# Layers written out instead of looped, and small VectorE operations given to ScalarE, in a two-layer decoder step

## The chip, the cores and the metric

The kernel runs on one core of one Trainium2 chip. The metric is the device time of one execution in microseconds (us). The engines are TensorE (PE in the profile; PEld is its weight load), VectorE (DVE), ScalarE (ACT), GpSimd (POOL) and SyncE (SP, which only issues DMAs). Each has its own instruction stream; they meet at semaphores.

## The reference

One inference step of a decoder of two layers for 256 prompt tokens and 8 sequences of 4 new tokens, 288 columns in all, model width 1024, fp32:

```python
for l in range(DEPTH):                       # DEPTH = 2
    z = x @ w_in                             # conv branch and attention branch
    u = ua * sigmoid(ug)                     # GLU, 512 channels
    A = silu(layer_norm(depthwise_conv31(u))) @ w_conv_out
    B = gated_sum(compressed, selected, window attention) @ w_attn_out
    m = sigmoid(g_a) * A + sigmoid(g_b) * B
    x = layer_norm(ALPHA * x + m @ w_o)
    x = layer_norm(ALPHA * x + (silu(x @ w_gate) * (x @ w_up)) @ w_down)
```

The old K and V rows lie in pages that a page table picks; the new K, V and convolution rows are outputs too.

## The kernel before

Everything is kept with channels on partitions and the 288 tokens as columns. Each fp32 operand of a big product is split into a rounded part and a rest (`w_hi`, `w_lo`; `x_hi`, `x_lo`), and a product is three matmuls (lines 717 to 719, 735 to 737, 754 to 756). Weights come in chunks of 128 x 1024: SyncE loads a chunk into one of three slots (`load_chunk`), ScalarE rounds it into `w_hi` (`high_part`, line 1129), GpSimd takes the rest into `w_lo` (`low_part`, four instructions of line 640), TensorE uses it. There are three `w_hi`/`w_lo` slots, so rounding chunk n waits until TensorE has finished chunk n-3.

**Order of work.** No planner: each engine's stream is written out by hand for one layer, and TensorE, VectorE, ScalarE and GpSimd run it in a hardware loop of two passes (`with layers(...)`, lines 647, 963, 1308, 1850). SyncE's stream has one pass in a loop and one behind it (lines 601 to 605). In a loop each `wait_ge` compares a semaphore with a value worked out from the register `layer`, and semaphores count on through both layers.

**First stage of a layer** (outputs 0 to 7 of `project_x`). TensorE multiplies the not yet normalised `xr_hi`/`xr_lo`, and VectorE corrects each result by mean and deviation. The outputs alternate between two PSUM banks, and output n+2 waits until VectorE has read output n out of its bank (line 1858). In VectorE's stream (lines 1886 to 1919) `norm_pair` normalises the residual, `fix_gate(c)` makes the gate's argument and `take_u(c)` makes `u`; ScalarE takes the tanh of the gate in between (`gate`, line 1333). `low_features` makes `x_lo`. Then come small operations on the layer's vectors `sm`: `nsa_hi`, `half_gb`, `alpha_gb` and two extra columns of `x_hi` (lines 1907 to 1918). After them VectorE works on the depthwise convolution (`convolve`, line 1602), with rotary steps between (`rope`, lines 1929 to 1936, which wait for TensorE's `turn`, line 996).

**Compression stage.** For five groups of rows (4, 0, 1, 2, 3, in this order) TensorE multiplies (`compress`, line 819), ScalarE copies half of the result (`h1_copy`), VectorE and ScalarE go to and fro for a GELU (`compress_dve`, line 1611, and `gelu_act`), and TensorE multiplies by the second weight (`second`, lines 833 to 840). On ScalarE the last group's `h1_copy(layer, 3)` (line 1399) stands behind copies into `v_tok` and `v_misc` and the DMA `kv_out` (lines 1389 to 1398). On TensorE two whole outputs (`fill`) stand between the fourth group's compression and `second(layer, 3)`; convolution statistics (line 774) follow. VectorE then copies the new tokens' queries into `qs_raw` and `qs_rot`, 16 copies of 64 x 32 (line 1952), which the attention over old rows needs first at line 913.

Of the kernel before, what the change touches and what calls it, by code (L numbers as in the profile page):

```python
# [19 lines left out]
F32 = mybir.dt.float32  # L20
# [9 lines left out]
TOKX = TOK + 2  # L30
# [117 lines left out]
def decoder_kernel(nc, xT, consts, page_table, weights, small, w1, w2, cmp_pages, slc_pages, win, past_u,  # L148
                   yT, kv_out, p_conv_out, s_conv_out, win_out):
    with ExitStack() as ctx:  # L150
# [141 lines left out]
        def s(name):  # L292
            return sm[:, SMALL[name]]
# [121 lines left out]
        rstd_copied = Signal("rstd_copied", 1)  # L415
        gate_fixed = Signal("gate_fixed", KC)
# [70 lines left out]
        def layers(eng):  # L487
            return eng.Fori(0, DEPTH)
# [5 lines left out]
        def _(sp):  # L494
# [107 lines left out]
            with sp.Fori(0, DEPTH - 1) as layer:  # L602
                body(layer, True)
                lead(layer + 1, False)
# [14 lines left out]
        def _(pool):  # L619
# [27 lines left out]
            with layers(pool) as layer:  # L647
# [39 lines left out]
        def _(pe):  # L687
# [275 lines left out]
            with layers(pe) as layer:  # L963
# [146 lines left out]
        def _(act):  # L1110
            owned = (act_order, conv_hi_ready, attn_hi_ready, hid_hi_ready, gates_act, hi_ready, x_hi_ready, gates_read, xc_ready, v_ready, h1_ready, hsq_ready, hth_ready, cmp_ready, squared, mean_squared, mean_copied, sd_ready,
                     swish_ready, gexp1, gwin_ready, gexp2, gpt_act, uexp, upt_ready, ax_ready, x_ready, ffn_tanh, raw_hi_ready, rstd_copied, gate_tanh)
# [195 lines left out]
            with layers(act) as layer:  # L1308
# [24 lines left out]
                def gate(n):  # L1333

                    act.wait_ge(*gate_fixed(layer, n + 1))
                    if n >= 2:
                        act.wait_ge(*u_taken(layer, n - 1))
                    do(sig_u[:, n % 2], gate_ps, ACT.Tanh, gate_tanh, wait=False, scale=0.5, bias=sums_of[:, 2, n % 2:n % 2 + 1])
# [18 lines left out]
                features_rounded(layer, 3)  # L1357
                chunk_read(4)
# [38 lines left out]
                act.wait_ge(*roped(layer, 2))  # L1397
# [158 lines left out]
        def _(dve):  # L1556
            v = nc.vector
            owned = (dve_order, conv_lo_ready, attn_lo_ready, hid_lo_ready, nsa_ready, x_lo_ready, x_sum, conv_ready, roped, qs_ready, hs_ready, hin_ready, hg_ready, centered, shifted, var_ready, sum_ready, square_sum_ready, normed, conv_act, gate_normed, hid_ready,
# [291 lines left out]
            with layers(dve) as layer:  # L1850
# [10 lines left out]
                def fix_gate(c):  # L1861

                    unshift_raw(2 * c, sums_of[:, 0])
                    do(v.tensor_scalar(sums_of[:, 2, c % 2:c % 2 + 1], sums_of[:, 0, 1:2], 0.5, None, ALU.mult), wait=False)
                    do(v.tensor_tensor(gate_ps, fixed_ps, rstd_sb, ALU.mult), gate_fixed)

                def take_u(c):

                    unshift_raw(2 * c + 1, sums_of[:, 1])
                    do(v.tensor_tensor(fixed_ps, fixed_ps, rstd_sb, ALU.mult))  # L1870
                    dve.wait_ge(*gate_tanh(layer, c + 1))
                    su = sig_u[:, c % 2]
                    do(v.tensor_scalar(su, su, 0.5, 0.5, ALU.mult, ALU.add))
# [33 lines left out]
                do(v.tensor_copy(nsa_hi[:], nsa_f))  # L1907
# [3 lines left out]
                do(v.tensor_scalar(half_gb[:], sm[:, SMALL["cg"].start:SMALL["cb"].stop], 0.5, None, ALU.mult))  # L1911
                do(v.tensor_scalar(alpha_gb[:], sm[:, SMALL["g1"].start:SMALL["b1"].stop], ALPHA, None, ALU.mult))
                g1, b1 = s("g1").unsqueeze(2), s("b1").unsqueeze(2)
                do(v.tensor_scalar(x_hi[:, :, TOK:TOK + 1], g1, -1.0, None, ALU.mult), wait=False)
                do(v.tensor_copy(x_hi[:, :, TOK + 1:TOKX], b1))
# [32 lines left out]
                for gg in range(2):  # L1948
                    rows = slice(64 * gg, 64 * gg + 64)
                    for src, dst in ((q_raw, qs_raw), (q_rot, qs_rot)):  # L1950
                        for hh in range(HG):
                            i = v.tensor_copy(dst[rows, :, gg, hh], src[rows, hh, SEQ:TOK].rearrange("p (b t) -> p b t", b=DEC_B))
                            do(i, qs_ready if gg and dst is qs_rot and hh == HG - 1 else None, wait=False)
# [122 lines left out]
                def raw_columns():  # L2076
# [156 lines left out]
```

## Time and profile before

| what | value |
|---|---|
| three runs | 1010.43, 1012.06, 1014.05 us (median 1012.06) |
| profiled execution | 1015.24 us |
| its span, first to last instruction | 1013.4 us |
| TensorE busy | 961.2 us (95%) |
| GpSimd busy | 752.4 us (74%) |
| VectorE busy | 653.0 us (64%) |
| ScalarE busy | 536.4 us (53%) |
| mean granted TensorE clock | 0.985 |

The shares are averages over a kernel with many stages. An engine that is busy for 95% of the span is the one to follow: what matters is where it isn't busy, what it waited for there, and where its clock was granted at half.

### The profile page before, as it was taken

To read this page: it belongs to the slowest core of one execution; us is meant where nothing else is said; L and a number is where in the kernel's file an instruction comes from. 1 tells how busy PE (TensorE), PEld (TensorE's weight loads), DVE (VectorE), ACT (ScalarE), POOL (GpSimd) and SP (SyncE) were. 2 spreads that over 40 slices of the span, in tenths; PEclk is the share of its full clock that TensorE was granted. 3 is DMA by queue.
4 is the path that set the end of the run, shared out by engine and by line. 5 is a ranking of instruction groups with operands and counts; after the bars stand their busy time and mean duration, and the time that the engine had idled before them with its cause. 6 is when DMAs were issued, how large, how long until landed. Compare 5 with 4: busy or idle time off the path is not lost.

```text
span 1013.4 us, 23246 instructions
## 1 busy us (share of the span) xinstructions
PE 961.2 (95%) x7294; PEld 912.0 (90%) x7294; DVE 653.0 (64%) x1476; ACT 536.4 (53%) x1000; POOL 752.4 (74%) x1081
## 2 busy tenths in 40 slices
PE   6898999989999999999989989999899999999995
PEld 5897888878999999999989978898799999999994
DVE  7999766566687555531469995855676765556035
ACT  5452475545575555544464426764556555555355
POOL 7787746443978888898877786455269888888986
PEclk9998999999999999999989999999999999999998
DMA  8885686822456764555457566776134454555543
GB/s 294 276 252 182 196 251 220 308 92 63 129 173 205 237 201 163 166 183 170 147 182 237 164 200 174 264 237 221 54 98 159 143 161 160 166 167 168 174 159 110
DMA packets 78916, 185.08 MB, mean 183 GB/s; under 512 B 9538, under 2 KB 42690, under 8 KB 78530
## 3 DMA queue, kind: packets, MB, share of 16 engines
q1 hardware_dynamic: 70288, 167.03, 50.6%
q10 hardware_dynamic: 8354, 15.59, 4.5%
q8 instruction: 62, 1.02, 0.4%
q0 software_dynamic: 144, 0.89, 0.2%
q14 instruction: 68, 0.56, 0.2%
HBM read 170.90 MB, written 12.57 MB: 181 GB/s over the span
## 4 chain that ended last, share of the span: by engine, by line
POOL 54%; issue 23%; PE 20%; ACT 1%; POOLq 1%; DVE 1%; DMA 0%; ACTq 0%; SPq 0%; DVEq 0%
POOL w_lo L640 47%; PE proj L717 5%; PE proj L718 4%; PE proj L719 4%; POOL hid L665 3%; POOL res L663 3%; PE proj L735 2%; PE proj L736 2%; PE proj L737 2%; DMA res<-xT_in 0%; POOLq L660 0%; POOLq L634 0%; ACT res L1134 0%; ACT xr_hi L1120 0%; POOL res L673 0%
## 5 line engine op out<-in xcount | busy, mean ns | idle before, releaser
L640 POOL TENSOR_TENSOR w_lo<-wch,w_hi 128x256 fp32r<-128x256 f32 x940 | 685.2, 764 | 245.2 <-ACT w_hi L1129 244.6
L717 PE MATMUL proj<-x_hi,w_hi 128*128 128x290 f32 (+1 forms) x1120 | 340.8, 304 | 2.8 <-ACT hid L1142 2.6
L718 PE MATMUL proj<-x_hi,w_lo 128*128 128x290 f32 (+1 forms) x1120 | 332.9, 297 | 0.0
L719 PE MATMUL proj<-x_lo,w_hi 128*128 128x290 f32 (+1 forms) x1120 | 332.1, 296 | 0.0
L1129 ACT ACTIVATE w_hi<-wch 128x1024 fp32r<-128x1024 f32 x235 | 247.8, 1055 | 130.1 <-PE proj L737 74.5
L717 PEld LDWEIGHTS proj<-x_hi,w_hi 128*128 128x128 f32 x1120 | 211.7, 189 | 6.6 <-issue 4.0
L718 PEld LDWEIGHTS proj<-x_hi,w_lo 128*128 128x128 f32 x1120 | 212.3, 190 | 0.6
L719 PEld LDWEIGHTS proj<-x_lo,w_hi 128*128 128x128 f32 x1120 | 212.3, 190 | 0.0
L735 PE MATMUL proj<-hid_hi,w_hi 128*128 128x288 f32 x352 | 104.3, 296 | 0.0
L737 PE MATMUL proj<-hid_lo,w_hi 128*128 128x288 f32 x352 | 103.6, 294 | 0.0
L736 PE MATMUL proj<-hid_hi,w_lo 128*128 128x288 f32 x352 | 103.3, 293 | 0.0
L1602 DVE SCALAR_TENSOR_TENSOR ps_s<-u_p,sm,ps_s 128x256 f32<-128x256 f32 x232 | 94.1, 483 | 3.8
L1688 DVE SCALAR_TENSOR_TENSOR res<-proj,res 128x288 f32<-128x288 f32 x32 | 14.6, 455 | 107.9 <-PE proj L737 93.0
L2096 DVE COPY sums_of<-proj 128x2 f32<-128x2 f32 x88 | 14.1, 160 | 95.3 <-PE proj L719 95.0
L736 PEld LDWEIGHTS proj<-hid_hi,w_lo 128*128 128x128 f32 x352 | 66.2, 188 | 0.1
L735 PEld LDWEIGHTS proj<-hid_hi,w_hi 128*128 128x128 f32 x352 | 66.1, 188 | 0.1
L737 PEld LDWEIGHTS proj<-hid_lo,w_hi 128*128 128x128 f32 x352 | 66.1, 188 | 0.0
L1134 ACT ACTIVATE q_raw<-q_raw,sums_of 128x288 f32<-128x288 f32 x44 | 23.6, 537 | 74.1 <-DVE q_raw L2109 74.1
L717 PE MATMUL proj<-xr_hi,w_hi 128*128 128x290 f32 x128 | 41.1, 321 | 17.6 <-POOL w_lo L640 9.7
L1134 ACT ACTIVATE res<-res,unit_top 128x128 f32<-128x128 f32 (+2 forms) x96 | 37.6, 393 | 27.7 <-DVE unit_top L1756 27.5
L717 PEld LDWEIGHTS proj<-xr_hi,w_hi 128*128 128x128 f32 x128 | 26.3, 205 | 19.2 <-DVE xr_lo_a L1578 9.7
L718 PE MATMUL proj<-xr_hi,w_lo 128*128 128x290 f32 x128 | 40.0, 312 | 0.0
(319 smaller groups left out, 1761.2 us busy)
## 6 DMA issues: line engine op xcount, KB each, us to landing
wch<-weights_in SPq DMA_DIRECT2D x235, 512.0 KB, 3.7
pg<-slc_pages_in SPq DMA_DIRECT2D x128, 128.0 KB, 2.4
pg<-cmp_pages_in SPq DMA_DIRECT2D x96, 128.0 KB, 3.1
wn<-win_in SPq DMA_DIRECT2D x16, 512.0 KB, 5.5
win_out<-wn ACTq DMA_DIRECT2D x4, 2048.0 KB, 9.7
pg<-cmp_pages_in ACTq DMA_DIRECT2D x32, 128.0 KB, 3.3
hid<-w_in SPq DMA_DIRECT2D x2, 1024.0 KB, 5.6
kv_out<-kv ACTq DMA_DIRECT2D x2, 864.0 KB, 4.4
```

Of the source, the lines that this page charges most:

```text
L640: last = nc.gpsimd.tensor_tensor(lo[:, cols], raw[:, cols], hi[:, cols].bitcast(F32), ALU.subtract)
L663: do(nc.gpsimd.tensor_tensor(dst, u_s[:, :, :, tap:tap + DEC_T], tap_weight(conv_w[:, :, tap]), ALU.mult))
L665: do(nc.gpsimd.tensor_tensor(out, out, tap_s[:], ALU.add))
L717: mm(ps, hi[:, kb], x_h[:, 0:n], start=kb == 0, stop=False)
L718: mm(ps, lo[:, kb], x_h[:, 0:n], start=False, stop=False)
L719: last = mm(ps, hi[:, kb], x_l[:, 0:n], start=False, stop=kb == KD - 1)
L735: mm(ps, hi, hid_hi[:, kb], start=kb == 0, stop=False)
L736: mm(ps, lo, hid_hi[:, kb], start=False, stop=False)
L737: last = mm(ps, hi, hid_lo[:, kb], start=False, stop=kb == KF - 1)
L1129: hi_ready.up(nc.scalar.activation(w_hi[:, n % PAIRS].rearrange("p k n -> p (k n)"), wch[:, n % SLOTS].rearrange("p k n -> p (k n)"), ACT. ...
L1134: i = nc.scalar.activation(out, in_, func, **kw)
L1602: i = v.scalar_tensor_tensor(out=out, in0=in_, scalar=conv_w[:, c, tap:tap + 1], in1=so_far, op0=ALU.mult, op1=ALU.add)
```

## The change

The four loops become Python loops, so that each engine's stream holds both layers one behind the other, and every wait compares with a constant. SyncE's loop of one pass is written out too. Counters of the signals are set back at each layer. In the first stage and behind the compression, work of VectorE goes to ScalarE. The halvings in `u` are arranged anew: ScalarE makes `1 + tanh` and VectorE multiplies by half of the deviation; to match, the extra column b2 of `xr_hi` is stored halved.

```diff
-        def layers(eng):
-            return eng.Fori(0, DEPTH)
+        def layers(signals):
+
+            for layer in range(DEPTH):
+                for sig in signals:
+                    sig.count = 0
+                yield layer
...
-            with sp.Fori(0, DEPTH - 1) as layer:
+            for layer in range(DEPTH - 1):
...
-            with layers(act) as layer:
+            for layer in layers(owned):
...
                 def gate(n):
...
-                    do(sig_u[:, n % 2], gate_ps, ACT.Tanh, gate_tanh, wait=False, scale=0.5, bias=sums_of[:, 2, n % 2:n % 2 + 1])
+                    do(sig_u[:, n % 2], gate_ps, ACT.Tanh, scale=0.5, bias=sums_of[:, 0, 1:2])
+                    do(sig_u[:, n % 2], sig_u[:, n % 2], ACT.Identity, gate_tanh, wait=False, bias=1.0)
...
                 features_rounded(layer, 3)
+                act.wait_ge(*small_in(layer, 1))
+                nsa_f = s("nsa").rearrange("p (c w) -> p c w", c=KD)
+                do(nsa_hi[:], nsa_f, ACT.Copy, wait=False)
+                do(x_hi[:, :, TOK:TOK + 1], s("g1").unsqueeze(2), ACT.Copy, wait=False, scale=-1.0)
+                do(x_hi[:, :, TOK + 1:TOKX], s("b1").unsqueeze(2), ACT.Copy, wait=False)
+                do(half_gb[:], sm[:, SMALL["cg"].start:SMALL["cb"].stop], ACT.Copy, wait=False, scale=0.5)
+                do(alpha_gb[:], sm[:, SMALL["g1"].start:SMALL["b1"].stop], ACT.Copy, small_copied, scale=ALPHA)
                 chunk_read(4)
...
-                act.wait_ge(*roped(layer, 2))
+                act.wait_ge(*roped(layer, 6))
+                for gg in range(2):
+                    rows = slice(64 * gg, 64 * gg + 64)
+                    for src, dst in ((q_raw, qs_raw), (q_rot, qs_rot)):
+                        for hh in range(HG):
+                            do(dst[rows, :, gg, hh], src[rows, hh, SEQ:TOK].rearrange("p (b t) -> p b t", b=DEC_B), ACT.Copy,
+                               qs_ready if gg and dst is qs_rot and hh == HG - 1 else None, wait=False)
...
                 def fix_gate(c):
...
-                    do(v.tensor_scalar(sums_of[:, 2, c % 2:c % 2 + 1], sums_of[:, 0, 1:2], 0.5, None, ALU.mult), wait=False)
...
                 def take_u(c):
...
-                    do(v.tensor_tensor(fixed_ps, fixed_ps, rstd_sb, ALU.mult))
+                    do(v.scalar_tensor_tensor(out=fixed_ps, in0=fixed_ps, scalar=0.5, in1=rstd_sb, op0=ALU.mult, op1=ALU.mult))
                     dve.wait_ge(*gate_tanh(layer, c + 1))
                     su = sig_u[:, c % 2]
-                    do(v.tensor_scalar(su, su, 0.5, 0.5, ALU.mult, ALU.add))
...
-                do(v.tensor_copy(nsa_hi[:], nsa_f))
+                dve.wait_ge(*small_copied(layer, 1))
                 do(v.tensor_tensor(nsa_lo[:], nsa_f, nsa_hi[:].bitcast(F32), ALU.subtract), nsa_ready)
                 fix_gate(3)
                 take_u(3)
-                do(v.tensor_scalar(half_gb[:], sm[:, SMALL["cg"].start:SMALL["cb"].stop], 0.5, None, ALU.mult))
-                do(v.tensor_scalar(alpha_gb[:], sm[:, SMALL["g1"].start:SMALL["b1"].stop], ALPHA, None, ALU.mult))
                 g1, b1 = s("g1").unsqueeze(2), s("b1").unsqueeze(2)
-                do(v.tensor_scalar(x_hi[:, :, TOK:TOK + 1], g1, -1.0, None, ALU.mult), wait=False)
-                do(v.tensor_copy(x_hi[:, :, TOK + 1:TOKX], b1))
...
                 compress_dve(layer, 3, fill=6)
-                for gg in range(2):
-                    rows = slice(64 * gg, 64 * gg + 64)
-                    for src, dst in ((q_raw, qs_raw), (q_rot, qs_rot)):
-                        for hh in range(HG):
-                            i = v.tensor_copy(dst[rows, :, gg, hh], src[rows, hh, SEQ:TOK].rearrange("p (b t) -> p b t", b=DEC_B))
-                            do(i, qs_ready if gg and dst is qs_rot and hh == HG - 1 else None, wait=False)
                 conv_center(layer)
...
-                    do(v.tensor_copy(xr_hi[:, :, TOK + 1:TOKX], b2))
+                    do(v.tensor_scalar(xr_hi[:, :, TOK + 1:TOKX], b2, 0.5, None, ALU.mult))
...
-                        do(v.tensor_tensor(lo[:, :, TOK + 1:TOKX], b2[:, blocks], xr_hi[:, blocks, TOK + 1:TOKX].bitcast(F32), ALU.subtract),
-                           wait=False)
+                        do(v.scalar_tensor_tensor(out=lo[:, :, TOK + 1:TOKX], in0=b2[:, blocks], scalar=0.5,
+                                                  in1=xr_hi[:, blocks, TOK + 1:TOKX].bitcast(F32), op0=ALU.mult, op1=ALU.subtract), wait=False)
```

## Rows read from the trace of the kernel before

**Rows 1.** The page's first part: busy time and share of each engine.

```profile
PE 961.2 (95%) x7294; PEld 912.0 (90%) x7294; DVE 653.0 (64%) x1476; ACT 536.4 (53%) x1000; POOL 752.4 (74%) x1081
```

**Rows 2.** The waits of TensorE: us in total, times, longest us.

```profile
PE proj L717 <- POOL w_lo L640: 11.1, 4, 9.7
PE ps_o L833 <- DVE res L1650: 5.2, 2, 2.6
...
PE proj L717 <- issue: 4.0, 1, 4.0
PE proj L717 <- DVE ps_t L1858: 4.0, 4, 1.5
```

**Rows 3.** Timeline between the layers: start, length, engine, line, operation, [idle before].

```profile
505.40 0.65 PE L796 MATMUL ps_s<-sq,cst 128*128 128x288 f32 x2
510.05 0.60 PE L717 MATMUL proj<-xr_hi,w_hi 128*128 128x290 f32 x1 [4.00 <-issue]
...
507.49 1.96 DVE L2128 RECIPROCAL ps_w<-sq 128x288 f32<-128x288 f32 x1 [0.60 <-ACT sq L1134]
513.12 0.76 DVE L1727 SCALAR_TENSOR_TENSOR res<-ps_s,res 128x576 f32<-128x576 f32 x1 [3.67 <-issue]
...
510.01 0.20 ACT L1134 ACTIVATE warm<-eps 128x1 f32<-128x1 f32 x1
...
510.47 2.79 POOL L640 TENSOR_TENSOR w_lo<-wch,w_hi 128x256 fp32r<-128x256 f32 x4
```

**Rows 4.** Busy time by stretch; PEclk is the granted clock, 1.00 the full one.

```profile
93.00:100.00 7.00, 6.46 (x20) 5.17 (x21) 6.74 (x18) 0.69 (x2) 5.98 (x14) 0.51 0.27 81
...
509.00:516.00 7.00, 5.95 (x24) 5.96 (x25) 1.97 (x3) 1.62 (x3) 4.25 (x6) 0.53 0.51 167
516.00:520.00 4.00, 4.00 (x31) 4.00 (x31) 3.16 (x8) 3.32 (x7) 2.18 (x4) 0.97 0.11 39
```

**Rows 5.** First stage of layer 0: timeline rows, and one group of small operations.

```profile
33.49 0.40 PE L717 MATMUL proj<-xr_hi,w_hi 128*128 128x290 f32 x1 [1.11 <-DVE ps_t L1858]
38.50 0.39 PE L717 MATMUL proj<-xr_hi,w_hi 128*128 128x290 f32 x1 [1.52 <-DVE ps_t L1858]
...
19.82 3.33 DVE L1873 TENSOR_SCALAR sig_u<-sig_u 128x288 f32<-128x288 f32 x1
27.94 0.31 DVE L1873 TENSOR_SCALAR sig_u<-sig_u 128x288 f32<-128x288 f32 x1
...
26.76 0.48 ACT L1134 ACTIVATE sig_u<-ps_t,sums_of 128x288 f32<-128x288 f32 x1
...
L1912 DVE TENSOR_SCALAR alpha_gb<-sm 128x16 f32<-128x16 f32 x2 | 1.3, 663 | 0.1
```

**Rows 6.** Timeline of layer 0 ahead of the compression: the fourth turn and its use.

```profile
82.92 0.65 PE L996 MATMUL ps_t<-q_raw,cst 128*128 128x288 f32 x2
...
84.39 0.45 DVE L1934 TENSOR_TENSOR sig_u<-ps_t,cst 128x288 f32<-128x288 f32 x1
```

**Rows 7.** Timeline of layer 0 around the last compression group.

```profile
119.03 2.04 ACT L1134 ACTIVATE v_misc<-ps_t 32x1024 f32<-32x1024 f32 x2
121.86 0.77 ACT L1134 ACTIVATE res<-ps_w 64x128 f32<-64x128 f32 x4 [0.79 <-PE ps_w L819]
...
127.25 0.68 DVE L1653 SCALAR_TENSOR_TENSOR res<-sq 64x512 f32<-64x512 f32 x1
...
128.40 0.44 PE L837 MATMUL ps_o<-res,w_sb 64*64 64x128 f32 x4
```

**Rows 8.** Groups of small ScalarE operations: busy us, mean ns of one, idle before.

```profile
L1134 ACT ACTIVATE kp_cmp<-ps_o 64x16 f32<-64x16 f32 x4 | 0.7, 178 | 0.4 <-ACT sq L1134 0.3
L1134 ACT ACTIVATE res<-ps_w 64x128 f32<-64x128 f32 x16 | 3.1, 271 | 3.9 <-PE ps_w L819 3.1 <-ACT v_misc L1134 0.8
L1134 ACT ACTIVATE warm<-eps 128x1 f32<-128x1 f32 x10 | 2.0, 203 | 0.1
```

**Rows 9.** The group of VectorE's query copies, same columns.

```profile
L1952 DVE COPY qs_raw<-q_raw 64x32 f32<-64x32 f32 x16 | 1.8, 173 | 0.1
```

More of the change, by code:

```diff
@@ L415, in decoder_kernel @@
         rstd_copied = Signal("rstd_copied", 1)
+        small_copied = Signal("small_copied", 1)
         gate_fixed = Signal("gate_fixed", KC)
@@ L646, in _ @@
             lo_ready.count = 0
-            with layers(pool) as layer:
+            for layer in layers((pool_order, lo_ready, conv_s_ready, half_centered)):
                 for n in range(PAIRS, EARLY + PAIRS):
@@ L961, in group_turn @@
                 gout_turned.up(pe.transpose(ps_o[:, P:2 * P], group_rows, k("ident")))
-            with layers(pe) as layer:
+            owned = (out_done, down_used, gates_turned, gout_turned, gates_done, turned, v_turned, h_done, w2_done, stat_done, spread_done, gm_done, gs_done, gsum_done, gt_done, gpv_done, us_done, ut_done, upv_done)
+            for layer in layers(owned):
                 state["out"] = 0
@@ L1111, in _ @@
             owned = (act_order, conv_hi_ready, attn_hi_ready, hid_hi_ready, gates_act, hi_ready, x_hi_ready, gates_read, xc_ready, v_ready, h1_ready, hsq_ready, hth_ready, cmp_ready, squared, mean_squared, mean_copied, sd_ready,
-                     swish_ready, gexp1, gwin_ready, gexp2, gpt_act, uexp, upt_ready, ax_ready, x_ready, ffn_tanh, raw_hi_ready, rstd_copied, gate_tanh)
+                     swish_ready, gexp1, gwin_ready, gexp2, gpt_act, uexp, upt_ready, ax_ready, x_ready, ffn_tanh, raw_hi_ready, rstd_copied, gate_tanh, small_copied, qs_ready)
             for sig in owned + (out_read[0], out_read[1], kv_stored, conv_stored, win_stored):
@@ L1307, in _ @@
             act.wait_ge(table_in, 16)
-            with layers(act) as layer:
+            for layer in layers(owned):
                 now["layer"] = layer
@@ L1557, in _ @@
             v = nc.vector
-            owned = (dve_order, conv_lo_ready, attn_lo_ready, hid_lo_ready, nsa_ready, x_lo_ready, x_sum, conv_ready, roped, qs_ready, hs_ready, hin_ready, hg_ready, centered, shifted, var_ready, sum_ready, square_sum_ready, normed, conv_act, gate_normed, hid_ready,
+            owned = (dve_order, conv_lo_ready, attn_lo_ready, hid_lo_ready, nsa_ready, x_lo_ready, x_sum, conv_ready, roped, hs_ready, hin_ready, hg_ready, centered, shifted, var_ready, sum_ready, square_sum_ready, normed, conv_act, gate_normed, hid_ready,
                      spread_read, gneg1, gm_read, gimp, gneg2, gp_ready, gpt_dve, gcopy_ready, go_ready, us_read, uneg, up_ready, uo_ready, mixed_ready, raw_lo_ready, sm_free, rstd_ready, gate_fixed, u_taken)
@@ L1848, in group_out @@
                     do(v.tensor_copy(dst, src), go_ready if g else None)
-            with layers(dve) as layer:
+            for layer in layers(owned):
                 now["layer"] = layer
```

## Prediction

> **What bounds the kernel.** First the engines' shares: TensorE is busy for 961.2 us of a span of 1013.4 [rows 1]. Some 52 us are left in which it stands still, and other engines count only where they cause these. Second, TensorE's waits [rows 2]: 9.7 of the 11.1 us for `w_lo` are the start of the kernel, which the change leaves as it is. The waits that the change touches are one of 4.0 us "for issue", in which nothing that the profile shows was missing; four, 4.0 us in all, for VectorE reading a bank (line 1858); and two, 5.2 us in all, for the first compression group (line 1650). Third, the timeline between the layers [rows 3]: the only "issue" wait is the loop's jump back. TensorE's last matmuls of layer 0 end at 506.05, the next starts at 510.05. VectorE stood 3.67 us after its reciprocal, also for "issue". Fourth, the granted clock [rows 4]. After the jump it was at half: 24 matmuls in 5.95 us between 509 and 516, against 31 in 4.00 us between 516 and 520. At 0.129 us each, 24 would take 3.1 us, so the low clock cost 2.9 us there. A like stretch follows the compression wait of layer 0 (0.51 from 93 to 100).
>
> **The jump.** With both layers written out there is no jump. The 4.0 us go if all that output 0 needs is there at 506.05: its weights were rounded before, and the last `xr_lo` block, which is not much later, is for the last eighth of the output only. So output 0 starts at once: -4.0. TensorE doesn't stand still, so I take the clock as staying at full: -2.9. What is late next is chunk 2. Its `w_lo` runs on GpSimd from 510.47 to 513.26 [rows 3], behind GpSimd's own subtraction, and none of that came from the jump. Outputs 0 and 1 (24 matmuls each at 0.135 us, some 3.25 us an output) end at 512.6, so TensorE waits 0.7 us. VectorE gets only 3.6 us earlier while TensorE gets 6.9 us earlier. I laid VectorE's steps of the first stage out again from 509.5 on with their old lengths less what is removed: output 6 starts without a wait, output 7 waits 0 to 1.4 us for its bank, as the four `low_features` ahead of it take very different times in the two layers. That is 0.7 in the middle, plus 0.3 for small ones, against 0.8 of wait there before (one of the four of [rows 2]): +0.2. ScalarE's restart, just after 510.21, is in time for all of this. Sum: -4.0 - 2.9 + 0.7 + 0.2 = -6.0. Ends: -2 (clock not regained, chunk 2 and 7 late) and -7.5 (no new wait). The waits' constants cost TensorE nothing: their arithmetic ran beside the queued matmuls, and is put at 0.
>
> **First stage, layer 0.** VectorE loses line 1873, four times 0.31 us, but one of them took 3.33 us at 19.82 [rows 5], four tiny ones of line 1864, and `nsa_hi`. ScalarE gains an Identity of about the tanh's length, 0.5 us, behind a finished tanh. The 3.0 us of the long one don't come through: the next `take_u` needs ScalarE's second tanh, which ran from 26.76 to 27.24, so the Identity ends near 27.9, where VectorE was at 27.94 anyhow. What is left is 0.31 a time: the waits of 1.11 and 1.52 us [rows 5] shrink together by 0.7. Taken: -0.7. Ends: -2.5 (nearly all of both) and +0.6 (the Identity late in each gate).
>
> **Small operations on `sm`.** Off VectorE come four at 0.2 to 0.7 us in the row of line 1912 and its neighbours, and `nsa_hi`; ScalarE gets five, some 0.2 us each by [rows 8], 1.1 us in all. They stand ahead of rounding chunk 7, and `w_lo` of chunk 7 would end about when output 7 starts: hidden, just. VectorE's new wait for them is met long before; behind it is only `nsa_lo`, which TensorE needs after output 7. VectorE's relief, 4 us by then, is mostly not worth its length either: its third and fourth `rope` need TensorE's turns. The fourth turn ended at 83.57 and VectorE used it at 84.39 [rows 6], so VectorE can gain 0.7 us on TensorE and no more. Both compression waits (2.6 us each, [rows 2]) shrink by that: -1.4. Ends: 0 and -1.4, and the half clock behind them may go as well (below). `raw_columns` keeps its count and shapes of instructions: 0.
>
> **The 16 copies on ScalarE.** They go ahead of `h1_copy(layer, 3)`. In layer 0 ScalarE's `v_misc` copies end at 121.07, `h1_copy(3)` starts at 121.86, VectorE's last step for this group ends at 127.93, and TensorE takes it at 128.40, right behind its two fills [rows 7]. So the slack is about 0.3 us. The new `roped(6)` wait costs 0: VectorE's `rope(5)` comes before its `compress_dve(2)`, thus before ScalarE's part of that group, which is before the copies. A 64x32 copy has no row: between 178 ns (64x16) and 271 ns (64x128), and 203 ns for a single column [rows 8]. Four of the 271 ns took 0.77 us, so they overlap, 0.17 apart. Taken 0.16 apart, 2.6 us for 16. Up to 0.3 us of it lies under the 0.79 us that ScalarE waited there. That leaves 2.3, less 0.3 of slack: 2.0 us of new TensorE wait in each layer, since convolution statistics and attention all stand behind it. VectorE's own copies, 173 ns each and overlapped [rows 9], lay ahead of `conv_center`, where it waits for TensorE: their going gives 0. Queued behind the copies are also `kv_out` (nobody waits for it soon) and the reading of two fills, first needed after `second(3)`. +4.0. Ends: +1.0 a layer (0.1 apart) and +3.7 a layer (0.25 apart, one after another), +2.0 and +7.4.
>
> A rule of the Trainium skill speaks against this part: "VectorE: DVE Perf Modes", section "The TRN2 errata", gives a ScalarE operation from SBUF to SBUF 224 cycles plus its elements, which would be an estimate of 213 ns a copy and 3.4 us for 16 without overlap. By it the term would be +5.6 rather than +4.0.
>
> **Sum.** -6.0 - 0.7 - 1.4 + 4.0 = -4.1 us. The profiled execution took 1015.24 (span 1013.4), 3.2 above the median of the three runs; a difference carries over, so 1012.06 - 4.1 = 1008.0.
>
> **Rivals.** The measurement tells 0.3%, 3.0 us, from no change.
>
> (a) The copies are hidden, or cheap, and a half-clock stretch behind a shortened wait goes. For it: the overlap at 0.17. Against: slack of 0.3 only. Copies +2.0, clock -2.9: near 1003. Chance 0.2.
>
> (b) The 4.0 us aren't the jump's: some other thing is late and the wait only changes its name. For it: "issue" names no cause. Against: VectorE shows it at the same place [rows 3], and TensorE in its whole trace nowhere else [rows 2]. Then -2.1 + 4.0, about 1014: no change. Chance 0.1.
>
> The Trainium skill, "Runtime: NRT & Kernel Launch", section "Instruction fetch mechanics", says that a taken branch outside the held pages makes the engine fetch before it can go on; by that rule (b) falls, and the trace's one "issue" wait agrees.
>
> (c) The clock moves about: a new wait of 2 us behind the fills is followed by half clock in one layer, +2.9. For it: of two equal waits before line 833 each was followed by some. Near 1011. Chance 0.12.
>
> (d) Slower: the copies run one after another, 3.7 us of wait a layer, and each such wait brings a half-clock stretch of 2.9 us: +13.2 against -8.1, 1017. It decides from some 0.25 us a copy on. For it: TensorE's longest other waits are shorter than 3.7. Against: ScalarE's small copies overlap. Chance 0.07.
>
> My forecast has the other 0.51. The range leaves out (d) and the tails: 1002.5 to 1013. Faster by over 0.3% are the forecast for the most part, (a), and a few of (c): 0.61. Same: the rest of the forecast, (b), most of (c): 0.32. Slower: 0.07.
>
> **What would show it.** Right: TensorE's waits have no "issue" row of 4 us; the clock at the layer boundary stays at 1.00; a short wait for `w_lo` at output 2 of layer 1; a new wait of about 2 us before line 837 in both layers, released by VectorE's line 1653, with `h1_copy(3)` as much later; compression waits of 1.9 rather than 2.6 us. Wrong: no wait at line 837 (copies hidden), or over 3 us there; a low clock at the boundary in spite of no standstill; a rise of the waits for `w_lo` in the first stage, which would mean that ScalarE's new work holds up the rounding of weights.

## The result and the profile after

The changed kernel takes 1002.95 us (median, 1002.45 to 1003.35), the kernel before beside it 1013.05: ratio 0.9898, 95% interval 0.9877 to 0.9918, so 10 us less, where 4.1 were forecast. The direction was right, and the time lies inside the range by 0.45 us at its lower end, but the size was less than half of what came. Of the four terms behind it one came out, and that one in part by luck, as is shown below. The profiled execution took 1003.35 us with a span of 1001.6, against 1015.24 and 1013.4 before.

The page's first part says where the 11.8 us of span came from: against [rows 1] TensorE's busy time fell by only 2.1 us, so 9.7 us are standstill.

```profile
PE 959.1 (96%) x7294; PEld 908.8 (91%) x7294; DVE 634.5 (63%) x1418; ACT 544.7 (54%) x1050; POOL 752.9 (75%) x1081
```

TensorE's waits in the changed kernel, same columns as [rows 2]:

```profile
PE proj L722 <- POOL w_lo L645: 13.8, 7, 9.9
PE ps_o L966 <- DVE sq L1857: 4.1, 2, 2.1
PE ps_o L842 <- DVE res L1673: 3.4, 4, 0.9
PE ps_s L941 <- DVE res L1772: 2.3, 2, 1.1
PE proj L722 <- ACT hid L1148: 1.8, 2, 0.9
PE ps_o L838 <- DVE res L1670: 1.2, 2, 0.7
PE ps_s L918 <- DMA pg<-slc_pages_in: 0.9, 1, 0.9
```

The "issue" row is gone. The two waits of 2.6 us for the first compression group (L833, now L838) are 1.2 us in all. The waits for VectorE's reading of a bank, 4.0 us before, have left the list, in part for waits for `w_lo` (11.1 to 13.8). The forecast new wait before the last compression group is there, but short: of the four waits of L842, two of 0.8 to 0.9 us stand before the first group that uses it and two, 0.89 and 0.73 us, before the last.

The clock by stretch, columns as [rows 4]; first fence the profiled execution of the changed kernel, second that of the same program run again later (below):

```profile
93.00:100.00 7.00, 6.16 (x37) 5.11 (x36) 6.83 (x16) 2.99 (x11) 6.06 (x13) 1.00 0.90 277
219.00:227.00 8.00, 8.00 (x45) 6.75 (x45) 4.74 (x16) 3.59 (x20) 0.00 (x0) 0.59 0.01 2
509.00:516.00 7.00, 6.85 (x51) 6.88 (x52) 5.16 (x12) 5.22 (x11) 6.25 (x10) 1.00 0.70 201
707.00:712.00 5.00, 5.00 (x33) 4.01 (x32) 3.79 (x10) 2.35 (x11) 0.00 (x0) 0.67 0.07 27
```

```profile
219.00:227.00 8.00, 6.92 (x58) 5.61 (x58) 6.08 (x17) 4.35 (x15) 0.58 (x1) 1.00 0.00 0
707.00:712.00 5.00, 4.09 (x34) 3.32 (x33) 3.97 (x11) 1.77 (x10) 0.00 (x0) 1.00 0.01 2
```

The stretches at 1.2 GHz of [rows 4], behind the compression wait and behind the jump, are at the full 2.4 GHz now. Two others came up behind the wait of 2.06 us before L966 in both layers, and the second execution has not even those.

**The positions.** Nothing so far says which part of the change did it. For that I read when TensorE starts the same matmul in both traces. Position is start in microseconds, in the timeline:

| TensorE's work | before | after | gained in the stage | forecast |
|---|---|---|---|---|
| layer 0: end of the first stage (start of `nsa`) | 42.27 | 38.77 | 3.50 | 0.7 |
| layer 0: first compression group (L833/838) | 93.54 | 87.94 | 2.10 | part of 1.4 |
| layer 0: next group (L837/842) | 104.55 | 96.88 | 2.07 | 0 |
| layer 0: last group (L837/842) | 128.40 | 121.66 | -0.93 | -2.0 |
| layer 0: last matmuls (L796/801) | 505.40 | 500.97 | -2.31 | 0 |
| layer 1: end of the first stage | 539.71 | 529.24 | 6.04 | 6.0 |
| layer 1: first compression group | 590.94 | 578.59 | 1.88 | part of 1.4 |
| end of TensorE's work | 1000.89 | 989.17 | -0.63 | -2.0 |

In these two traces the boundary came out as forecast to the tenth, the copies at less than half, and the first stage and the compression groups at several times their terms. The last row holds more than the copies of layer 1: 0.66 us are gained up to the next group, 0.70 lost up to the last (at 624.56 before and 612.25 after), and 0.59 lost behind it. The 2.07 us of the third row are the half clock of [rows 4] from 93 to 100, priced there by the like stretch at 2.9, less a new wait of 0.84. Of the 2.31 us lost in the fifth, 1.60 are in this execution alone, with its low clock from 219 to 226; the second execution, which has no low clock there, still loses 0.71, although the kernel before had 3.4 us of half clock in the same stage (154.4 to 157.8). Nothing here places this remainder.

### The profile page after: what moved, and what is told of

It reads as the page before. It is cut to its first block, busy times and chain, and to the rows that moved or that the text cites. A ratio compares the mean times of both kernels' runs of the same rounds, so it can differ in the third digit from the quotient of the medians.

```text
span 1001.6 us, 21268 instructions
## 1 busy us (share of the span) xinstructions
PE 959.1 (96%) x7294; PEld 908.8 (91%) x7294; DVE 634.5 (63%) x1418; ACT 544.7 (54%) x1050; POOL 752.9 (75%) x1081
## 4 chain that ended last, share of the span: by engine, by line
PE 72%; DVE 8%; ACT 6%; SPq 5%; POOL 4%; issue 3%; DMA 2%; ACTq 0%; DVEq 0%
PE proj L722 16%; PE proj L723 15%; PE proj L724 15%; PE proj L740 5%; PE proj L741 5%; PE proj L742 5%; POOL w_lo L645 3%; ACT res L1140 3%; SPq L518 2%; SPq L532 2%; PE ps_o L891 1%; ACT w_hi L1135 1%; PE proj L759 1%; DMA wch<-weights_in 1%; DVE ps_s L1622 1%
## 5 line engine op out<-in xcount | busy, mean ns | idle before, releaser
L1140 ACT ACTIVATE hid_hi<-ps_s 128x288 fp32r<-128x288 f32 x44 | 18.1, 411 | 43.5 <-DVE ps_s L2128 43.5
L722 PE MATMUL proj<-mix_hi,w_hi 128*128 128x288 f32 x128 | 38.2, 298 | 1.6 <-POOL w_lo L645 1.6
```

The costliest lines, as they stand in the source:

```text
L722: mm(ps, hi[:, kb], x_h[:, 0:n], start=kb == 0, stop=False)
L1140: i = nc.scalar.activation(out, in_, func, **kw)
```

## The experiments

**The theories.** A, the one on record: the layer jump carries the gain and the waits' constants are worth nothing. B: with the layers written out each wait's value is a constant, which was expected to shorten every hand-over between VectorE and ScalarE by a tenth of a microsecond or two, and to pay where TensorE waits for a chain of them. C came up when the first traces were compared: where the half-clock stretches lie, and a long instruction or two, are accidents of one execution.

All ratios are to runs of the kernel before on the same chip. It took 1012.41, 1014.40 and 1013.73 us in the three sets (the first four runs, the next four, the last four).

### The two halves of the change alone

**The loops written out, nothing else.**

```
-        def layers(eng):
-            return eng.Fori(0, DEPTH)
+        def layers(signals):
+            for layer in range(DEPTH):
...
```

> The kernel before with its loops written out and nothing else. Theory A (the prediction's: writing out saves the jump alone, register arithmetic of the waits costs nothing): -6.0 us, all of it between the layers; the first stage of layer 0 and the waits before lines 833 (2.6 us), 936 (1.13) and 961 (2.33) stay as before. Theory B (each hand-over between engines also gets some 0.1 us shorter, since the wait's value no longer has to be worked out): -7.5 to -9 us, the wait before 961 falls to about 2.06 in both layers and the first stage of layer 0 gets shorter too.

Measured: 1005.48 us, ratio 0.9937 (0.9918 to 0.9957). That is 6.4 us less, between the two theories, and the interval holds both.

**The small operations moved, every loop kept.** The diff is the change without the lines above.

> The changed kernel with its loops kept: only the moved operations. Theory A: -5 us (3.5 in the first stage of layer 0, 1.4 or more before line 833, less 1 us a layer for the query copies), the wait of 4.0 us for issue and the half clock behind it stay. Theory B: -2 to -4 us, because part of what the first stages gained in the changed kernel is due to the constants; the wait before 961 stays 2.33. Rival: the copies on ScalarE eat it up, within 1 us of no change.

Measured: 1014.02 us, ratio 1.0009 (0.9990 to 1.0027). Neither theory had this; the rival came nearest.

Each alone does about what the terms of the forecast say: 6.4 us for the loops (forecast: the boundary's 6.0), and nothing measurable for the small operations (forecast: -0.7, -1.4 and +4.0, some 2 us slower). Together they do 10.3 by the same kind of ratio. The halves' ratios add to 0.9946, give or take 0.0027, where the whole has 0.9898: some 5 us, give or take 3, come only with both. So most of the miss is in having added terms from a trace in which VectorE and ScalarE were late. TensorE's waits with the loops alone written out:

```profile
PE ps_o L965 <- DVE sq L1842: 4.1, 2, 2.1
PE ps_o L837 <- DVE res L1655: 3.1, 2, 1.6
PE proj L721 <- DVE ps_t L1863: 1.9, 2, 0.9
PE ps_o L841 <- DVE res L1658: 1.8, 2, 0.9
```

The wait before the first compression group is 1.6 us here, not 2.6, with no operation taken from VectorE, and the one before the turn of the gate's outputs (L961 before, L965 here) is 2.06 instead of 2.33. That is what B says and A doesn't. The first stage of layer 0 ends at 38.54, ahead of any jump, where it ended at 42.27 before and at 40.18 in another kernel with loops and the same instructions up to there (the copies alone moved, below).

### Which engine's loop

**TensorE's loop alone put back.**

```
-            for layer in layers(owned):
+            with loops(pe) as layer:
                 state["out"] = 0
```

> The changed kernel with TensorE's loop alone kept. If TensorE's own jump is what stands between the layers: the 4.0 us wait for issue is back, a stretch at half clock behind it (2.9 us), minus the 1.1 us wait for w_lo that the changed kernel has there: +5 to +6 us against the changed kernel, thus near 1008.5. If the other engines' jumps set it: within 1.5 us of the changed kernel (1003), with less than 1 us for issue.

Measured: 1005.44 us, ratio 0.9932 (0.9911 to 0.9953). The wait for issue came back, but the time lies between the two that were expected, 1008.5 and 1003.

**VectorE's and ScalarE's loops alone put back.**

```
-            for layer in layers(owned):
+            with loops(act) as layer:
...
-            for layer in layers(owned):
+            with loops(dve) as layer:
```

> The changed kernel with the loops of VectorE and ScalarE alone put back; TensorE, GpSimd and SyncE stay written out. Theory B (the constants in the waits of VectorE and ScalarE carry most of the gain, since each hand-over between them is shorter; TensorE's own jump is worth about 4 us of idle time): the kernel with TensorE's loop alone put back took 1005.4 us and the one with all loops put back 1014.0, so this one has TensorE's jump gone (no wait named issue at 498 to 508 us), but VectorE's jump of 3.7 us is back and TensorE waits some of it out behind the boundary, and the chain of waits before the turn of the gate's outputs is 2.5 us again, not 2.06: 1008 to 1012 us. Theory A (TensorE's jump alone carries the gain, as forecast): no more than 1 us above the changed kernel, 1003 to 1004 us, with that chain at 2.06 us.

Measured: 1015.46 us, ratio 1.0015 (0.9998 to 1.0032): the whole gain is gone, although TensorE has no jump; this is more than B expected. First fence TensorE, second VectorE of this kernel at the boundary, third TensorE with only its own loop back:

```profile
513.46 0.41 PE L724 MATMUL proj<-xr_hi,w_hi 128*128 128x290 f32 x1 [3.33 <-DVE ps_t L1880]
```

```profile
511.15 0.76 DVE L1749 SCALAR_TENSOR_TENSOR res<-ps_s,res 128x576 f32<-128x576 f32 x1 [4.00 <-issue]
```

```profile
502.02 0.60 PE L724 MATMUL proj<-xr_hi,w_hi 128*128 128x290 f32 x1 [4.11 <-issue]
```

TensorE's 4.11 us come back with its loop. Without it, and with VectorE's, TensorE starts the next layer at once (503.36) and then stands 3.33 us for a bank that VectorE reads late, because VectorE itself jumped for 4.00 us. From the last matmuls of layer 0 to the end of layer 1's first stage it takes 34.31 us before, 33.45 with all loops and the small operations moved, 33.02 with TensorE's loop alone, 32.69 with VectorE's and ScalarE's, and 28.27 with none (28.76 in the second execution). The two jumps overlap: take either away and 0.4 to 0.8 us are gained, take both and some 5. The small differences are no more than two executions differ by: the kernel before with the query copies alone moved (below) takes 33.00 us here, against 34.31, with 3.4 us of half clock at the boundary against 6.8. Writing out every loop but TensorE's (1.0009 to 0.9932) gains 7.8 us, most of it within the layers: the next stage shows a part. GpSimd's and SyncE's loops are in this, too, but with VectorE's and ScalarE's kept, writing out the other three gains nothing (1.0015). My term for the boundary came near because I had laid VectorE's steps out without its jump as well; by "TensorE's 4.0 us of issue" alone it would have been wrong.

The Trainium skill, "Runtime: NRT & Kernel Launch", section "Instruction fetch mechanics", has a taken branch outside the held pages cost the engine a fetch. The rows agree that the engine stands at its jump, for 3.67 to 4.13 us on either engine; they don't show what it does in that time.

### The stage between the first stage and the compression

This stretch shows where the halves meet. TensorE needs, from the start of `nsa` to the first compression group:

| kernel | layer 0 | layer 1 |
|---|---|---|
| before | 51.27 | 51.23 |
| small operations moved, all loops kept | 49.50 | 51.27 |
| the same, TensorE's loop written out | 49.41 | 51.18 |
| loops written out alone | 50.25 | 50.28 |
| changed kernel, TensorE's loop put back | 49.30 | 49.25 |
| changed kernel | 49.17 | 49.35 |

In layer 0 the halves give 1.8 and 1.0 us, and together 2.1. In layer 1 they give nothing and 1.0, and together 1.9. Over both layers that is 3.7 against 4.0, so the greater part of what comes only with both lies elsewhere, for some 2.4 us in the query copies (below); the rest isn't placed.

Small operations moved, with loops: VectorE in layer 1, at the fourth turn.

```profile
574.90 3.23 DVE L1624 SCALAR_TENSOR_TENSOR ps_s<-u_p,sm,ps_s 128x256 f32<-128x256 f32 x8
578.04 0.45 DVE L1950 TENSOR_TENSOR sig_u<-ps_t,cst 128x288 f32<-128x288 f32 x1
578.41 0.93 DVE L1951 TENSOR_TENSOR q_rot<-q_raw,cst 128x288 f32<-128x288 f32 x1
579.37 0.86 DVE L1952 TENSOR_TENSOR q_rot<-q_rot,sig_u 128x288 f32<-128x288 f32 x1
```

The changed kernel, VectorE in layer 0 at the same place and on to the first compression group:

```profile
80.10 0.46 DVE L1948 TENSOR_TENSOR sig_u<-ps_t,cst 128x288 f32<-128x288 f32 x1 [0.89 <-PE ps_t L1002]
80.48 0.45 DVE L1949 TENSOR_TENSOR q_rot<-q_raw,cst 128x288 f32<-128x288 f32 x1
80.96 0.46 DVE L1950 TENSOR_TENSOR q_rot<-q_rot,sig_u 128x288 f32<-128x288 f32 x1
84.90 0.52 DVE L1642 SCALAR_TENSOR_TENSOR sq<-ps_w,h_bias,res 64x30 f32<-64x30 f32 x2
85.45 0.88 DVE L1622 SCALAR_TENSOR_TENSOR ps_s<-u_p,sm,ps_s 128x256 f32<-128x256 f32 x2
86.24 0.33 DVE L1662 SCALAR_TENSOR_TENSOR sq<-sq 64x64 f32<-64x64 f32 x1
86.60 0.88 DVE L1622 SCALAR_TENSOR_TENSOR ps_s<-u_p,sm,ps_s 128x256 f32<-128x256 f32 x2
```

And the same steps before:

```profile
84.75 0.84 DVE L1935 TENSOR_TENSOR q_rot<-q_raw,cst 128x288 f32<-128x288 f32 x1
85.62 0.87 DVE L1936 TENSOR_TENSOR q_rot<-q_rot,sig_u 128x288 f32<-128x288 f32 x1
90.06 0.52 DVE L1622 SCALAR_TENSOR_TENSOR sq<-ps_w,h_bias,res 64x30 f32<-64x30 f32 x2
90.69 0.88 DVE L1602 SCALAR_TENSOR_TENSOR ps_s<-u_p,sm,ps_s 128x256 f32<-128x256 f32 x2
91.48 0.28 DVE L1642 SCALAR_TENSOR_TENSOR sq<-sq 64x64 f32<-64x64 f32 x1
91.91 0.88 DVE L1602 SCALAR_TENSOR_TENSOR ps_s<-u_p,sm,ps_s 128x256 f32<-128x256 f32 x2
```

Three things are to be seen. First, in the changed kernel VectorE waits 0.89 us for TensorE's turn: it has caught up, as forecast, and 0.8 us is all that this can give. Behind its own jump, in layer 1 with loops, it isn't caught up: no wait before 578.04, although TensorE's fourth turn was over at 577.31, and the small operations taken off it buy nothing. Second, the two `q_rot` steps take 0.45 and 0.46 us instead of 0.84 and 0.87, another 0.8 us that no term had. GpSimd's rows tell what the earlier steps miss: before, its subtractions for `w_lo` (L640) run from 84.55 to 85.28 and from 85.23 to 86.17, and each step starts beside one of them and ends 0.31 or 0.32 us behind it. After, the steps start at 80.48 and 80.96, in a pause of GpSimd from 78.61 to 81.05. The same holds throughout: in the traces of all 14 runs, 93 rotary steps take over 0.8 us, and every one ends 0.31 to 0.32 us behind a GpSimd instruction that was running when it started. Third, the gap behind a VectorE instruction when the next one waits for a semaphore that is already met: 90.58 to 90.69 and 91.76 to 91.91 before, 85.42 to 85.45 and 86.57 to 86.60 after, 0.11 and 0.15 us against 0.03 each. In each gap of before, VectorE's queue has one register operation (at 90.61 and 91.81, 0.04 us each), and after it has none. That is what the constant saves, some 0.1 us a gap. It is VectorE's own restart that got shorter and not the way over to ScalarE, as B had it: ScalarE starts 0.09 us behind the signal in both (90.58 to 90.67, and 85.42 to 85.51). From the fourth turn's end to the first compression group it was 9.97 us (83.57 to 93.54) and is 7.87 (VectorE's start at 80.10, less the 0.03 of a gap, to 87.94): 2.1 us less, of which 0.8 the earlier start, 0.8 `q_rot`, and 0.5 these gaps and VectorE's shorter last `res` step.

### The query copies

**The copies alone moved, in the kernel before.**

```
-                act.wait_ge(*roped(layer, 2))
+                act.wait_ge(*roped(layer, 6))
+                for gg in range(2):
...
+                            do(dst[rows, :, gg, hh], src[rows, hh, SEQ:TOK]..., ACT.Copy, ...)
```

> The kernel before, with its loops, and of the change the move of the 16 query copies to ScalarE alone. As forecast, 2.0 us per layer at the wait before the last turn of compression, which goes from 0.3 to 1.6 or more, less what VectorE's relief gives later in the layer: 1012 to 1017 us, with that wait at 1.6 us as in the kernel with all the small operations and the loops. Rival (the copies are no part of that 1.6 us; the gate's operations on ScalarE delay it): the wait stays under 0.5 us and the time is that of before, 1013.

Measured: 1016.08 us, ratio 1.0018 (1.0001 to 1.0035). ScalarE's and TensorE's rows at the last group of layer 0, and below them the changed kernel's:

```profile
118.21 0.59 ACT L1134 ACTIVATE qs_raw<-q_raw 64x32 f32<-64x32 f32 x4
120.38 0.77 ACT L1134 ACTIVATE res<-ps_w 64x128 f32<-64x128 f32 x4
126.60 0.43 PE L837 MATMUL ps_o<-res,w_sb 64*64 64x128 f32 x4 [1.59 <-DVE res L1659]
```

```profile
113.27 0.59 ACT L1140 ACTIVATE qs_raw<-q_raw 64x32 f32<-64x32 f32 x4
114.85 0.56 ACT L1140 ACTIVATE qs_rot<-q_rot 64x32 f32<-64x32 f32 x4
115.44 0.77 ACT L1140 ACTIVATE res<-ps_w 64x128 f32<-64x128 f32 x4
121.66 0.43 PE L842 MATMUL ps_o<-res,w_sb 64*64 64x128 f32 x4 [0.89 <-DVE res L1673]
```

The copies take 2.14 us for 16 in both, from the first start to the last end, 0.134 us a copy where I took 0.16. From `h1_copy(3)` to TensorE's use it is 6.22 us in both, and was 6.54 before (121.86 to 128.40, [rows 7]): a slack of 0.32, as forecast. In the kernel with loops the copies make a wait of 1.59 us, and against the kernel before, the stretch from the first use of L837 to the last grows by 1.67 us in layer 0 and 2.15 in layer 1: the forecast's 2.0 a layer. In the changed kernel ScalarE starts them just ahead of TensorE's third group (113.27 against 113.31), where with loops it starts 0.66 us behind it (118.21 against 117.55). ScalarE is earlier in its chain by that much, and so the wait is 0.7 us shorter. Against the loops alone written out (23.84 us from the first use to the last in both layers) the copies cost 0.94 and 0.80 us in the changed kernel (24.78 and 24.64). With all small operations and the loops it is 26.00 and 25.96 against 23.85 and 23.94 before, so 2.15 and 2.02: 2.4 us more in all. The Trainium skill's figure ("VectorE: DVE Perf Modes", "The TRN2 errata"), from which I had estimated 213 ns a copy, holds for one copy: they take 208 to 230 ns each, with a median of 213. What made 3.4 us of it was that I added 16 of them without overlap. In the trace they overlap, with starts 0.12 to 0.14 us apart but for one gap of 0.24.

**The copies put off**, behind `second_out(layer, 3)` on ScalarE:

> The changed kernel with the 16 query copies put behind second_out(layer, 3) on ScalarE rather than ahead of h1_copy(layer, 3). If they cause the new waits of 0.89 and 0.74 us before the last second weight: these go, and -1.5 to -2 us against the changed kernel (1001 to 1001.5). Rival: the convolution squares and the root behind them on ScalarE get later by the 2.1 us of the copies, and the wait only moves to line 774's second group: 1003 to 1005.

Measured: 1001.77 us, ratio 0.9903 (0.9878 to 0.9927). The ratio isn't below the changed kernel's 0.9898.

**The copies back on VectorE**, the rest of the change kept, twice in different sets:

> The changed kernel with the 16 query copies back on VectorE ahead of the normalisation's centring. Theory B (the move to ScalarE cost 0.89 and 0.74 us of TensorE's time before the last turn of compression and took nothing from it elsewhere, as VectorE's copies lay beside TensorE's work): both those waits go, no other wait grows by more than 0.3 us, 1001 to 1002 us, as with the copies put off. Rival: VectorE's relief by 16 times 0.173 us per layer is what lets the attention's first stages start on time, and TensorE waits for VectorE there again: 1004 to 1006 us, with a new wait on VectorE between 135 and 160 us.

Measured: 1002.20 us, ratio 0.9888 (0.9864 to 0.9911).

> The candidate for a version better than both: the changed kernel with the 16 query copies on VectorE, as before. Theory B: it lacks the waits of 0.89 and 0.74 us before the last turn of compression, 1.0 to 1.5 us faster than the changed kernel beside it. Rival: the two can't be told apart, under 0.5 us.

Measured: 1003.14 us, ratio 0.9892 (0.9864 to 0.9919), and the changed kernel beside it:

> The changed kernel once more, beside the three that follow on the same chip: 1003 us, 0.988 to 0.991 of the kernel before, with the waits and the stretches of half clock of its first trace. If the stretches of half clock lie elsewhere in this second profiled execution of the same program (Theory C: where they fall is an accident of the execution), up to 3 us of every difference so far says nothing; if they lie where they lay (219.5 and 707.6 us, Theory B), they belong to the program's order of work.

Measured: 1001.87 us, ratio 0.9884 (0.9859 to 0.9910). Its trace has no stretch of half clock but the tail, so C holds for where these stretches lie.

In all three runs without the copies ahead of the last group its wait is gone, and in all three nothing is gained that can be measured. A part of the gain may go into another wait, for the pages of the selected blocks, which come by a DMA. Queries put off:

```profile
PE ps_o L842 <- DVE res L1673: 1.8, 2, 0.9
PE ps_s L918 <- DMA pg<-slc_pages_in: 1.2, 1, 1.2
```

It is 1.2 to 1.3 us in these three, 0.9 in the changed kernel's first trace and absent from its second, so this is not shown. The move of the copies could be left out with no measurable loss, and no version tried measurably beats the changed kernel.

### The gate's operations and the small vectors

**The gate's halving and shift back on VectorE:**

```
-                    do(sig_u[:, n % 2], gate_ps, ACT.Tanh, scale=0.5, bias=sums_of[:, 0, 1:2])
-                    do(sig_u[:, n % 2], sig_u[:, n % 2], ACT.Identity, gate_tanh, wait=False, bias=1.0)
+                    do(sig_u[:, n % 2], gate_ps, ACT.Tanh, gate_tanh, wait=False, scale=0.5, bias=sums_of[:, 2, n % 2:n % 2 + 1])
...
```

> The changed kernel with the halving of the gate's bias, the shift of the tanh's result and the copies of the raw columns back on VectorE as before. Theory B (with written-out waits VectorE is still what TensorE waits for in the first stage, so its four small operations cost some 0.2 us each there): the waits on VectorE in the first stage and ahead of the compression grow by 0.5 to 1.5 us in each layer, 1004 to 1006 us. Rival (these operations are hidden by TensorE's matmuls and only the loops count): 1003 us, waits as in the changed kernel.

Measured: 1007.05 us, ratio 0.9922 (0.9897 to 0.9948). This is 1 us beyond B's figure. The first stages take 1.0 and 0.7 us more than in the changed kernel's first trace, as B had it (`nsa` at 39.79 against 38.77, the boundary 28.92 against 28.27). But of the 4.0 us by which the span is longer, 3.6 come behind the last compression group of layer 1, where the clock is at half for 10.2 us from 707.8 on, against 3.4 in the changed kernel. So the ratio can't be put down to the gate's operations alone.

**The small vectors back on VectorE** (`nsa_hi`, `half_gb`, `alpha_gb`, two columns of `x_hi`):

> The changed kernel with the copies of the small vectors (the centred ones, the halved and the scaled gains and biases, the two columns of x_hi) back on VectorE. Theory B: the long VectorE instruction of 3.33 us beside GpSimd's tensor_tensors comes back in the first layer alone, and TensorE's first wait of layer 0 moves from 0.7 to 2 or 3 us; in layer 1 GpSimd is elsewhere and nothing changes: 1004 to 1006 us. Rival (hidden in both layers): 1003 us.

Measured: 1004.33 us, ratio 0.9910 (0.9887 to 0.9934). The expectation had one thing wrong: the instruction of 3.33 us didn't come back in layer 0. It is one of the gate's, not of these, and it turns out below to belong to one execution.

**The gate's operations alone on top of the loops:**

> Loops written out, and of the small operations the gate's alone (no halving of the bias column on VectorE, the shift of the tanh's result on ScalarE); query copies and small vectors stay on VectorE. Theory B: the gate's operations are the part of the small operations that pays, by 2 to 3 us against the loops alone (1005.5): 1002.5 to 1003.5 us, the waits ahead of the first turns of compression at 0.5 and 0.84 us. Rival (it is the small vectors that pay): 1005 us, with the wait of the first layer at 0.9 us on VectorE.

Measured: 1003.13 us, ratio 0.9899 (0.9874 to 0.9925). The time is B's; of the waits, layer 0 has the 0.5 and 0.84 us, while layer 1's first is still 1.57.

Against the loops alone (0.9937) the gate's operations give 0.4%, all that the small operations give. Without them, the changed kernel loses 0.3%. The intervals of these pairs overlap, so neither is shown, though both point the same way; and the second pair differs in the clock, as said. The traces don't place it in one wait. With the gate's part moved, the first stage of layer 1 shows the boundary at 28.86 us against 29.36, and `nsa` to compression in layer 0 at 49.15 against 50.25; in layer 1 it is 50.25 against 50.28. The small vectors are worth 0.1 to 0.3%, which these runs don't tell from nothing.

## Why the prediction was right and wrong

**The jump: right in its mechanism, to the tenth by luck.** -6.0 forecast, -6.04 in the table of positions. The term of 2.9 for the clock came from a boundary with 6.8 us of half clock. Two other kernels with all loops have 3.4 us there and need 33.00 and 33.45 us rather than 34.31, and the changed kernel's second execution 28.76 rather than 28.27. By these the boundary is worth 4.2 to 6.0 us. The half clock behind the jump went too: the row from 509 to 516 has 1.00 and 51 matmuls, where [rows 4] has 0.53 and 24. What was late next was as said: a wait for `w_lo` (1.14 us before 509.15, forecast 0.7 at output 2) and 0.30 us for a bank (0.89 in the second execution). Rival (b), the wait that only changes its name, is out for the changed kernel. It is just what happens if VectorE's loop stays.

**The constants: the step that failed.** It reads "The waits' constants cost TensorE nothing: their arithmetic ran beside the queued matmuls, and is put at 0". It looks at TensorE's own queue only and was never asked of VectorE and ScalarE, where a wait stands between two dependent steps. A row of the trace of before would have told it: 0.11 to 0.15 us between 90.58 and 90.69, and again between 91.76 and 91.91, with nothing to wait for. One execution has 1978 instructions less (23246 to 21268): 2465 register operations are gone, and 647 plain semaphore waits have come. With the loops alone written out the way from `nsa` to the compression is shorter by 1.0 us in each layer, with no operation of VectorE moved, and the first stage of layer 0 ends 1.6 us earlier than in the trace with loops that lacks the long step (38.54 against 40.18, one execution each). No jump has gone before in layer 0, so there it isn't the jump. These 3.6 us were put at 0. The step also reached into the other terms: the compression waits and the copies were priced from where VectorE and ScalarE stood in the kernel with loops, and these are the terms that came out at 4.0 for 1.4 and at 1.6 for 4.0.

**First stage of layer 0: mis-sized**, -0.7 against -3.5. "The 3.0 us of the long one don't come through" was argued, and wrong. The kernel before with only the query copies moved runs the same instructions up to there. In its trace the same step is short, and `nsa` starts 2.09 us earlier, at 40.18:

```profile
19.10 0.67 DVE L1879 TENSOR_SCALAR sig_u<-sig_u 128x288 f32<-128x288 f32 x1
25.60 0.86 DVE L1879 TENSOR_SCALAR sig_u<-sig_u 128x288 f32<-128x288 f32 x1
```

So the 3.33 us of [rows 5] belong to the one execution that I read, and 2.1 of the 3.5 us are no part of the change. The reason given, that `take_u` needs ScalarE's second tanh at 26.76 anyhow, fails because the tanh moves too: it starts at 25.02 here. Some 0.7 us of the difference were there ahead of the long step (18.05 against 18.76 for the reading of the bank before it). The long one, from 19.82, ends at 23.15, 0.18 us behind the last of eight subtractions that GpSimd ran one behind the other (17.37 to 22.97). This is also why the two profiles lie 11.9 us apart and the medians 10.1.

**Compression waits: mis-sized**, -1.4 against -4.0 (2.10 and 1.88). "VectorE can gain 0.7 us on TensorE and no more" was right for when VectorE starts on the fourth turn. It took everything behind that start as of fixed length, and there another 1.3 us a layer lay, in `q_rot` beside GpSimd and in the gaps.

**The copies: mis-sized by a state, not by their price**, +4.0 against +1.6 (0.89 and 0.73). With loops the term measured 1.67 and 2.15 us, as forecast. In the changed kernel ScalarE comes to them earlier. The price of one copy, 0.16, was 0.134.

**Rivals.** Rival (a) came nearest (1003, chance 0.2), with the half clock behind the compression wait gone (0.51 to 1.00) and copies at less than +2.0, but by a mechanism that it doesn't name. Rival (c), the clock that moves about, holds as an observation. The changed kernel's first trace has two low stretches, 10.2 us, and the second none; the trace of before has 20.5 us of them, the tail left out. Over all executions it is no accident, though. The mean granted clock was 0.986 to 0.988 in every kernel whose VectorE and ScalarE kept their loops (over 12 to 22 executions each) and 0.991 to 0.994 in every other. By the last set it was 0.9876 of a span of 1012.0 before, and 0.9938 of 1000.1 after, which is 25.1 and 12.4 us at half clock, 12.7 less. [Rows 4] price 6.8 us of it at 2.9, so some 5 of the 12 us of span are the clock, an estimate from these rows. It goes with the standstills, fewer waits of 2.6 us and fewer stretches at 1.2 GHz, but no run changed one without the other. Rival (d) had no sign in any trace: the copies overlap.

**The sum.** In the profile: 6.0 for the boundary, 3.5 for the first stage, 4.0 for the compression groups, less 1.6 for the copies, is 11.9 against 11.8 of span; the stretch of half clock that went from layer 0 and what came in its place cancel within it. It closes for these two executions. Between the medians it is 10.1 us, as 2.1 of the first stage and a part of the boundary's clock are the one trace's.

**Left open.** Where some 2 of the 5 us lie that come only with both halves. Why the changed kernel's busy time on TensorE fell by 2.1 us and not by the 4.4 that the 10.3 us less of half clock would give. And how the constants and the absence of a jump divide VectorE's part of the gain in layer 1: writing a loop out gives both there.

## What to carry to other kernels

Two jumps that lay side by side were worth 0.4 to 0.8 us one by one, no more than two executions differ by, and some 5 together: look for the engine that stands at the same place before pricing either. Price a wait on a register's value on the engines that pass work to and fro, not on the one that has a queue; it shows in the trace as a gap of 0.11 to 0.15 us behind an instruction, where a constant leaves 0.03. When a VectorE step takes 0.87 us in one place and 0.45 in another, look at GpSimd's rows beside it. And before a long instruction of a trace is priced, ask for a second execution of the same program: here one execution's long step and late start were worth 2 us, as much as a whole term.

## What was not expected of the hardware

A jump costs VectorE as much as TensorE, 3.67 to 4.13 us against 3.93 to 4.11, and TensorE's first matmuls behind its own show the low clock. Sixteen ScalarE copies of 64x32 between buffers of SBUF, of 208 to 230 ns each, need 2.14 us. The same VectorE instruction, 128x288 in and out, took 3.33, 0.67, 0.55 and 0.31 us in different executions and places; the 3.33 ended with GpSimd's row of eight subtractions. Rotary steps of 0.45 us took over 0.8 us 93 times, and each time they ended 0.31 to 0.32 us behind a GpSimd instruction. And the granted clock, averaged over executions, went with the waits that the other two engines cause on TensorE, by 0.6%.
